# Prompt attention of a decoder step: 16 query tiles from position 16 on, meta tokens in the samples' tile, keys through memory, one mask, blocks turned in twos

## What is computed

```python
qa, ka, va, qi, ki, wi, qb, kb, vb, fl = split(h @ w_in)          # 1024 -> 2000 columns
# A: the indexer scores every key; each query keeps the 256 best admissible ones
sc  = einsum('bqhk,bqh->bqk', relu(einsum('bqhd,bkd->bqhk', qi, ki) * 64 ** -0.5), wi * 8 ** -0.5)
idx = top_k(where(kpos <= qpos, sc, -inf), 256)
oa  = softmax(qa . ka[idx] * 64 ** -0.5) . va[idx]                # 8 heads, one key head
# B: all keys, with a sum of forget gates as bias
ob  = softmax(qb . kb * 64 ** -0.5 + (c_q - c_k)) . vb            # 8 heads, two key heads
h   = layer_norm(ALPHA * h + [oa ; ob] @ w_o)
h   = layer_norm(ALPHA * h + (silu(h @ w_gate) * (h @ w_up)) @ w_down)
return h[:, 16:], ...                                             # meta tokens' rows are dropped
```

## Time and profile before

| | us |
|---|---|
| median of 3 runs | 5134.49 |
| lowest and highest | 5130.62, 5140.98 |
| the profiled execution, its own time | 5144.56 |
| its span | 5142.9 |
| projection, until attention's first instruction | 632.8 |
| attention | 1999.9 |
| decode | 661.4 |
| mix_out | 283.3 |
| feed-forward | 1565.5 |

### The profile page before, as it was taken

One profiled execution on the slowest core, in us unless ns is written; L12 is line 12 of the kernel. 1 busy time (PEld: TensorE's weight loads), 2 busy tenths in 40 slices (PEclk: granted clock), 3 DMA queues, 4 the chain that ended last, 5 costly groups with the idle time before them and its releaser, 6 DMA issues. The chain is left out here.

```text
span 5142.9 us, 61315 instructions
## 1 busy us (share of the span) xinstructions
PE 4384.8 (85%) x22926; PEld 3111.6 (61%) x22926; DVE 2775.2 (54%) x5067; ACT 1823.3 (35%) x2724; POOL 544.6 (11%) x699
## 2 busy tenths in 40 slices
PE   7999666777777777887878789797999999999997
PEld 3444334444444444454445554343999999999997
DVE  2222158887889999999822321144335334353443
ACT  1323233343444444454444334201323333232331
POOL 0111111010000000000036752000000000000000
PEclk9999867777888999999989888798999999999998
DMA  3222211000000000000046773133444444445442
GB/s 125 91 91 81 77 46 35 20 27 20 20 21 21 18 18 23 24 9 16 5 165 197 218 239 132 66 110 116 118 137 114 130 121 124 135 121 141 114 125 69
DMA packets 458486, 447.44 MB, mean 87 GB/s; under 512 B 22568, under 2 KB 402736, under 8 KB 457994
## 3 DMA queue, kind: packets, MB, share of 16 engines
q1 hardware_dynamic: 408090, 267.19, 18.1%
q0 software_dynamic: 50176, 177.32, 10.1%
HBM read 377.21 MB, written 67.22 MB: 86 GB/s over the span
## 5 line engine op out<-in xcount | busy, mean ns | idle before, releaser
L469 DVE TENSOR_SCALAR_CACHE_REDUCE at_relu<-at_scores,at_cand 128x384 f32<-128x384 f32 (+14 forms) x480 | 741.2, 1544 | 9.4
L1350 PE MATMUL ff_ps<-ff_h_high,ff_w_high 128*128 128x416 f32 x1760 | 619.3, 352 | 25.8 <-DVE ff_w_low L1444 25.8
L1352 PE MATMUL ff_ps<-ff_h_high,ff_w_low 128*128 128x416 f32 x1760 | 622.1, 353 | 0.0
L1351 PE MATMUL ff_ps<-ff_h_low,ff_w_high 128*128 128x416 f32 x1760 | 615.3, 350 | 0.0
L858 ACT ACTIVATE at_pT_sb<-tr 128x512 f32<-128x512 f32 x612 | 357.9, 594 | 446.4 <-PE tr L755 446.2
L304 PE MATMUL pP<-w_in,hT 128*128 128x500 f32 x1088 | 472.1, 590 | 30.7 <-ACT hT L352 19.0
L845 ACT ACTIVATE at_probs<-at_probs,at_nmax 128x128 f32<-128x128 f32 (+16 forms) x272 | 341.2, 1255 | 419.6 <-DVE at_nmax L923 418.8
L1444 DVE TENSOR_TENSOR ff_w_low<-ff_w_raw,ff_w_high 128x2048 fp32r<-128x2048 f32 (+1 forms) x150 | 375.6, 2505 | 188.9 <-ACT ff_w_high L1399 188.9
L1399 ACT ACTIVATE ff_w_high<-ff_w_raw 128x2048 fp32r<-128x2048 f32 (+1 forms) x150 | 311.6, 2078 | 361.7 <-PE ff_ps L1352 359.7
L755 PE MATMUL tr<-ident,at_probs 128*128 128x128 f32 x2448 | 422.2, 303 | 12.1 <-ACT at_probs L845 12.1
L735 PE MATMUL S<-kbT,at_queries_b 73*128 73x512 f32 (+3 forms) x720 | 346.8, 622 | 93.1 <-DVE at_nmax L923 54.5
(11 more groups left out here) (291 smaller groups left out, 6439.7 us busy)
## 6 DMA issues: line engine op xcount, KB each, us to landing
ff_w_raw<-in_w_gate SPq DMA_DIRECT2D x110, 512.0 KB, 3.9
ff_w_raw<-in_w_up SPq DMA_DIRECT2D x110, 512.0 KB, 5.2
ff_w_raw<-in_w_down SPq DMA_DIRECT2D x80, 704.0 KB, 6.0
out_PN<-pn POOLq DMA_DIRECT2D x17, 1000.0 KB, 6.4
at_q_raw<-dram_QTA SPq DMA_DIRECT2D x132, 128.0 KB, 2.9
x_in<-in_x_rows SPq DMA_DIRECT2D x17, 512.0 KB, 3.6
dram_HN<-x_in POOLq DMA_DIRECT2D x17, 512.0 KB, 6.3
dram_QTA<-qaiT POOLq DMA_DIRECT2D x17, 512.0 KB, 4.9
```

Source lines behind the costliest of these rows:

```text
L469: return v.tensor_scalar(out, x, cand.bitcast(F32), 0.0, ALU.is_ge, ALU.add, accum_out=cnt)
L1350: pe.matmul(out, w_high[p][:, w], high, start=first, stop=False)
L1351: pe.matmul(out, w_high[p][:, w], low, start=False, stop=False)
L1352: return pe.matmul(out, w_low[p][:, w], high, start=False, stop=last)
```

## The change

The attention has 16 tiles of 128 queries, which begin at position 16; the meta tokens' own outputs aren't returned, and are no longer attended. Tile t has W = 128 (t+1) + 16 keys. The rows are ordered anew: tile 0 of projection holds meta tokens, samples and padding, tiles 1 to 16 the prompt. All stages but attention keep 17 tiles; feed-forward covers 2048 + 8 columns.

```diff
 def spans(width):
-    return [(c, min(SPAN, width - c)) for c in range(0, width, SPAN)]
+    parts = -(-width // SPAN)
+    each = -(-width // (16 * parts)) * 16
+    return [(c, min(each, width - c)) for c in range(0, width, each)]
 def width(t):
-    return (t + 1) * P
+    return (t + 1) * P + N_META
-        FIRST_TOPK = TOPK // P
+        FIRST_TOPK = TOPK // P - 1
-GCOLS = -(-ALL // (2 * GROUPS)) * 2
+GCOLS = -(-(SEQ + N_SAMPLE) // (2 * GROUPS)) * 2
```

```diff
-                for k, (high, low) in enumerate(((ka_high, ka_low), (ki_high, ki_low))):
-                    ch.step(v.tensor_copy(high[:, ds(t * P, P)], pQ[:, 0, k * P:(k + 1) * P]))
-                ch.wait()
...
+                if not is_first(t):
+                    v.wait_ge(k_stored, 32 * t)
+                ch.step(v.tensor_copy(kT[:, 0:2], pQ[:, 0, 0:2 * P].rearrange("p (a n) -> p a n", a=2)))
+                ch.step(v.tensor_copy(kT[0:AUG, 2:4], pQ[0:AUG, 0, 2 * P:4 * P].rearrange("p (a n) -> p a n", a=2)))
                 ch.wait()
                 v.sem_inc(q_evac, 1)
```

```diff
+                pool.dma_start(KTD[0:2, :, ds(at, m)].rearrange("a p n -> p a n"), kT[:, 0:2, 0:m]).then_inc(k_stored, 16)
+                pool.dma_start(KTD[2:4, 0:AUG, ds(at, m)].rearrange("a p n -> p a n"), kT[0:AUG, 2:4, 0:m]).then_inc(k_stored, 16)
```

```diff
+                for two in pairs(blocks):
...
+                    ready = state["turned"]
+                    for kb in two:
+                        turn(n, lambda h: probs[:, grp, h, kb * P:(kb + 1) * P])
...
+                        turn_sums_and_late(n, slot, lambda h: probs[:, grp, h, nb * P:nb * P + N_META])
+                        ready = state["turned"]
+                    for done, copied, at in ready:
+                        wait(pe, tr_copied, copied)
...
+                    if over:
+                        wait(pe, tr_copied, n["tr"].at(-1))
```

**The rest.** decode clears `sampT` (now a part of `work`, 1024 columns) and stores whole rows of tile 0:

```diff
-                sp.dma_start(MT[row:row + P, :].rearrange("p (c n) -> p c n", n=P)[:, :, N_META:N_META + NB], sampT[:])\
-                    .then_inc(stored, 16)
+            sp.dma_start(MT[0:P, :], work[:, 0:8 * P]).then_inc(stored, 16)
...
+            v.memset(sampT, 0.0).then_inc(cleared, 1)
```

More of the change, by code:

```diff
@@ L508 @@
 SPAN = 1024
+TURNED = 4
 class Tally:
@@ L575, in attend @@
         wi = [sb(f"wi{p}", [P, HEADS]) for p in range(2)]
-        mask = sb("mask", [P, ROWS])
-        scores = [sb(f"scores{p}", [P, ROWS]) for p in range(2)]
+        mask = sb("mask", [P, TOTAL])
+        scores = [sb(f"scores{p}", [P, TOTAL]) for p in range(2)]
         cand = sb("cand", [P, 1], I32)
@@ L598, in attend @@
         wi_here = sem("wi_here")
-        mask_here = sem("mask_here")
+        mask_here = [sem(f"mask_here{part}") for part in range(2)]
         s_full = sem("s_full")
@@ L613, in attend, with pairs @@
         COUNTS = ("full", "relu", "acc", "topk", "ttr", "exp", "tr", "pvs", "norm")
-        FIRST_TOPK = TOPK // P
+        FIRST_TOPK = TOPK // P - 1
+        def pairs(blocks):
+            blocks = list(blocks)
+            return [blocks[i:i + 2] for i in range(0, len(blocks), 2)]
         def units(t):
@@ L644, in share, with mask_of, load_keys @@
             return range(nb * j // parts, nb * (j + 1) // parts)
+        def mask_of(t):
+            return mask[:, TOTAL - width(t):TOTAL]
+        def load_keys(queue, to, k, signal, first, last):
+            rows = to.shape[0]
+            queue.dma_start(to[:, first:last], KTD[k, 0:rows, first:last]).then_inc(signal, 16)
         block = ctx.enter_context(nc.Block())
@@ L719, in _ @@
         def _(pe):
-            state = dict(kind="ttr", run=0, group=0, tb=0, block=0)
+            state = dict(kind="ttr", run=0, group=0, tb=0, block=0, turned=[], ends=1)
             n = {k: Tally() for k in COUNTS}
@@ L768, in turn_sums @@
                 ins.then_inc(tr_full, 1)
-                n["tr"].add()
+                for h in range(4):
+                    ins = pe.matmul(tr[state["tb"] % 2][0:N_META, 2, h * LATE:(h + 1) * LATE], late(h), ident[:, P - LATE:P],
+                                    start=True, stop=True)
+                ins.then_inc(tr_full, 1)
+                n["tr"].add(2)
+                state["ends"] = 2
                 state["tb"] += 1
@@ L795, in weigh @@
                         ins.then_inc(pv_step, 1)
-                    if kb == nb - 1:
+                    state["turned"] = state["turned"][len(ready):]
+                    if over:
+                        wait(pe, tr_copied, n["tr"].at(-1))
+                        late_probs = pT[0:N_META, state["block"] % TURNED, 0:4 * LATE].rearrange("p (c e n) -> p e c n", e=2, n=LATE)
+                        for e in range(2):
+                            ins = pe.matmul(pv[bank][e * HD:(e + 1) * HD, :, P - LATE:P], values(nb, N_META), late_probs[:, e],
+                                            start=False, stop=True)
+                        ins.then_inc(pv_step, 1)
+                        state["block"] += 1
@@ L899, in tile @@
                     indexer(t)
-            for t in range(TILES):
+            for t in range(QT):
                 tile(t)
-            copies(range(TILES), TILES, n)
+            copies(range(QT), QT, n)
         @block.vector
```

239 lines of the change are left out of this document (144 added, 95 removed).

## The result

The changed kernel takes **4939.25 us** (median of 4 runs, 4938.44 to 4946.88) against 5137.73 of before (median of 4 runs on the same chip); the ratio is **0.9622**, 95% interval 0.9608 to 0.9635. Forecast were 4899 and a range of 4850 to 4980. The direction and the range held; 198 us were gained, not 236.

What follows compares the result with a forecast made beforehand. DVE's columns and waits were taken to bound attention's tiles 2 to 15, PE projection and feed-forward. Attention -212, projection -12, decode +1 and feed-forward -13 sum to -236: 5134.5 to 4899 us, range 4850 to 4980.

Steps and rivals of the forecast that it cites:

- rival E: Attention's middle: PE granted its lower clock (0.5), kernel slower at 5408 us; decides below clock 0.575; chance 0.03.
- a) Columns: Attention's middle: each tile has 112 columns less on DVE's path, 7.29 us a tile, -104 us.
- b) Mask and relus: Attention's middle: one mask and equal units remove DVE's waits but 22 of 90.8 us, -69 us.
- c) Waits for S: Attention's middle: of DVE's 20.2 us of waits for S, -8 us, between 0 and -20.
- Half a microsecond in the differences: Base of the forecast: profiled execution 0.2% off the median, making half a microsecond in differences worked out on the profile.
- d) Start: Attention's start: only tile 0 precedes the first choosing tile, which starts after 60 us instead of 77.3, -17 us.
- e) Last tile: Attention's last tile: first half -4.8 us (DVE's), second half -9.2 us (PE's), together -14 us.
- f) Projection: Projection: two copies of 256 columns replace one copy of 1.49 us, 0.72 us less in 17 tiles, -12 us.
- g) Feed-forward: Feed-forward: four columns less at 0.42 ns a column over 7920 products, -13 us.
- Rival B: Attention's middle: PE takes over, mask and relu waits become waits for S, 4976 us; chance 0.17.
- D: Attention's start: gives nothing, as hops behind each other eat tile 0, 4916 to 4926 us; chance 0.12.

Runs made afterwards that it cites:

- e6: Kernel before with one mask for all tiles, loaded once, each tile taking its slice: ratio to before 0.9953, 5109.83 us.
- e8: Kernel before with both one mask for all tiles and units of equal size: ratio to before 0.9883, 5074.56 us.
- The three part kernels: Kernel before with one mask, with equal units, and with both: 5109.83, 5105.54 and 5074.56 us, beside 5134.79 of before.
- e11: e2 with POOL's far keys and mask loaded only after A's queries of tile 1 are split, second far half later still: ratio to before 0.9582, 4925.65 us.
- e5: Changed kernel with blocks turned and multiplied one by one instead of in twos: ratio to before 0.9628, 4942.1 us.
- e4: Changed kernel with the uneven units of before (1024 columns and the rest) instead of equal ones: ratio to before 0.9718.
- e3: Changed kernel with the candidate instruction taking one tensor and a scalar operand, in all bisection steps but first and last: ratio to before 0.9601, 4933.4 us.
- e1: Changed kernel with B's queries of tile 1 loaded ahead of A's raw queries in SP's queue: ratio to before 0.9619, 4943.47 us.
- e2: Changed kernel with each 73-row load from SP's queue made in pieces of 64 and 9 rows: ratio to before 0.9581, 4924.05 us.

## Why the prediction was right, and where it was off

- **What bounds the kernel** was read rightly: the middle shrank with DVE's columns and waits, and PE's granted clock (0.86 on the mean of the middle, before 0.84) was far from rival E's 0.575.
- **a) Columns, -104.** By kind of instruction, in tiles 1 to 14 against 2 to 15: passes with their likes 55.6 us less, logits 26.2, index scores 12.8, the rest of `choose` 8.5: 103.1, against 104 forecast. But `at_cand`'s instructions took 4.7 us more, as DVE was held by POOL more often, and DVE's busy time fell by 97.0 (rows that overlap counted once).
- **b) Mask and relus, -69.** Right in kind (e6, e8) and sized well: 61.3. What stays is not 1.6 us a tile but 2.1 (29.5 us in 57 waits), since the second and third relu are a little late as well.
- **c) Waits for S, -8.** Measured -6.4, but that can't be told from chance: in four kernels with PE's columns unchanged they were 4.3 to 20.2 us.
- **The base.** The three part kernels have middles 36.5, 38.7 and 73.4 us shorter than the profiled before, while their medians are 25.0, 29.3 and 60.2 lower. The waits for mask and relus alone shrink by 20.5, 32.6 and 60.3 us, near the medians; what the middles have beyond that is in the main waits for `S` (15.9, 6.6 and 11.7 less). So some 10 us of the profiled middle seem to be of that one execution (its mean clock is 0.910, theirs 0.916 to 0.919); no second profile of before shows it. "Half a microsecond in the differences" was too little by these 10 us: gains were read in a slower execution and taken off a median that doesn't have its waits. Of the forecast's own terms only c's 8 us can be such waits.
- **d) Start, -17.** -13.8. The hops up to the second split were right (indexer's queries split at 38.5 us, forecast 42.5), but B's queries of tile 1 took 20.9 us from issue to use instead of 15: their first packet came 7.6 us after the issue (2.1 in before), behind the far keys. With the far keys issued later and the rows in pieces the first packet came after 1.5 us (e11). The prediction had asked of the far keys only whether they would be late themselves, not whom they would delay.
- **e) Last tile, -14.** Measured -5.8. The second part came out (-8.6 for -9.2): the blocks gave 5.6 (e5) for 5.5, the equal units 1.5 (e4) for 4. The first part failed, +2.8 for -4.8. The prediction counted DVE's columns and half a microsecond for equal units there, and no wait. But DVE waited 9.3 us for `S` instead of 1.6, since blocks in twos (3.1 us, e5) and equal units (2.8 us, e4) both bring a head's products later.
- **f) Projection, -12.** -12.1, with PE's wait at 0.59 as forecast (0.6). The copies were not tried apart.
- **g) Feed-forward, -13.** -9.5, by the pace of the four columns from 416 to 412.

Rival B did not come: the waits that went were not taken over by `S`. D had its mechanism (loads that eat the shorter tile 0), at a smaller price.

## What to carry to other kernels

Price a group of instructions of a saturated engine with its shape's slope, and it comes out to a per cent; price waits with care, since their size in one profiled execution can be 10 us off. An engine's busy time can hide waits: look for instructions of one shape with durations of their own (0.16 and 2.2 us) and for what else ends when they end. And when a transfer is added at a place where others are awaited, ask whom it delays, and how many rows it has.

## What the runs showed of the hardware that was not expected

A DVE instruction with two tensors in SBUF stood still until POOL's instruction was through, up to 2.2 us for one of 0.16 (39 of 39 cases; none with one tensor, e3). The form with a tensor as scalar operand took 0.21 us for 0.16. A load of 73 rows (292 KB) from SP's queue took 15.7 us alone, its 73 packets one after the other 0.155 us apart, and 21 to 30 us beside the far keys (e1); the same rows as 64 + 9 were through in 1.8 us and let PE start 16 us sooner (e2). Products of 384, 412 and 416 columns, at a granted clock of 0.98 on the mean of the stage, were paced at 175.1, 187.75 and 188.9 ns.
